# Moving the first expert's down product ahead of the slots' names and the third gather

## What is computed

```python
def hier_moe(x, w_group, w_router, w_gate, w_up, w_down):
    g_logits = (xt @ w_group)                      # 4 groups, the best one is taken
    ...
    e_top, e_idx = lax.top_k(e_logits, 2)          # 2 of its 8 experts
    e_w = jax.nn.softmax(e_top, axis=-1) * g_w
    ...
    hid = jax.nn.silu(xblk @ w_gate[e]) * (xblk @ w_up[e])      # 1024 -> 512
    return hid @ w_down[e]                                      # 512 -> 1024
```

## Time and profile before

| | us |
|---|---|
| median of 3 runs | 1673.22 (1672.76 to 1675.41) |
| profiled execution, own time | 1668.99 |
| its span | 1667.0 |
| TensorE busy | 1592.2 (96%) |
| VectorE busy | 486.2 (29%) |
| ScalarE busy | 356.8 (21%) |

### The profile page before, as it was taken

How to read it: one execution, slowest core, us unless ns; L and a number is a source line. 1 busy time by engine, 2 the same in 40 slices (tenths; PEclk the granted TensorE clock), 3 DMA queues, 4 the chain that set the end, 5 groups by cost and what they waited for, 6 DMA issues and landing times.

```text
span 1667.0 us, 21128 instructions
## 1 busy us (share of the span) xinstructions
PE 1592.2 (96%) x7988; PEld 754.5 (45%) x7988; DVE 486.2 (29%) x1252; ACT 356.8 (21%) x835; POOL 197.6 (12%) x298
## 2 busy tenths in 40 slices
PE   7999899899999999999899989999899999999995
PEld 4545574433333333333446447865433333333332
DVE  1485751621111111111412235652611111111114
ACT  2445351301111111111200235642111111111110
POOL 2240320000000000000101012330000000000000
PEclk9999999999999999999999999999899999999998
DMA  8620217379999999999914120034699999999997
GB/s 239 254 100 7 85 21 303 134 299 421 422 422 421 421 422 423 422 422 400 348 14 173 66 54 1 1 138 166 254 416 422 421 421 422 422 422 421 422 422 314
DMA packets 118312, 474.20 MB, mean 284 GB/s; under 512 B 40821, under 2 KB 47221, under 8 KB 68332
## 3 DMA queue, kind: packets, MB, share of 16 engines
q1 hardware_dynamic: 110156, 456.98, 68.5%
q10 hardware_dynamic: 3136, 8.40, 1.3%
q0 software_dynamic: 4960, 8.04, 1.3%
HBM read 454.84 MB, written 26.77 MB: 289 GB/s over the span
## 4 chain that ended last, share of the span: by engine, by line
PE 75%; SPq 11%; DMA 5%; DVE 5%; issue 2%; ACT 1%; POOL 1%; DVEq 0%; POOLq 0%; ACTq 0%
PE bank L1845 19%; PE bank L1858 9%; SPq L1791 9%; PE bank L1473 8%; PE bank L1818 8%; PE bank L550 7%; PE bank L844 6%; PE bank L438 4%; DMA arena<-in_moe_w_up 3%; PE bank L403 3%; PE bank L1833 2%; SPq L1800 2%; PE bank L925 2%; PE bank L420 2%; DVE arena L2354 1%
## 5 line engine op out<-in xcount | busy, mean ns | idle before, releaser
L1845 PE MATMUL bank<-arena 128*64 128x512 f32 x2048 | 454.3, 596 | 9.3 <-DMA arena<-in_moe_w_up 5.8
L1845 PEld LDWEIGHTS bank<-arena 128*64 128x64 f32 x2048 | 144.2, 138 | 306.7 <-issue 293.6
L1858 PE MATMUL bank<-arena 128*64 128x512 f32 x1024 | 230.6, 592 | 2.1 <-DVE arena L1951 2.1
L1947 DVE TENSOR_TENSOR arena<-arena,bank 128x256 f32<-128x256 f32 x64 | 26.9, 421 | 644.5 <-ACT arena L1937 644.5
L1818 PE MATMUL bank<-arena 128*64 128x512 bf16 x1280 | 164.8, 388 | 1.9 <-DVE arena L1813 1.9
L1864 POOL DMA_INDIRECT y_d<-arena,slot_row x62 | 60.7, 979 | 864.2 <-ACT arena L1942 837.0
L1473 PE MATMUL bank<-arena 128*128 128x512 f32 x320 | 138.1, 593 | 0.8 <-ACT arena L320 0.8
L1858 PEld LDWEIGHTS bank<-arena 128*64 128x64 f32 x1024 | 71.8, 137 | 124.2 <-issue 110.6
L1937 ACT ACTIVATE arena<-bank 128x256 f32<-128x256 f32 x64 | 24.5, 383 | 415.2 <-PE bank L1845 415.2
L550 PE MATMUL bank<-arena 128*128 128x512 f32 x256 | 111.9, 594 | 0.0
L844 PE MATMUL bank<-arena 128*128 128x512 f32 (+1 forms) x288 | 105.3, 525 | 0.0
(11 more groups left out here) (305 smaller groups left out, 1455.4 us busy)
## 6 DMA issues: line engine op xcount, KB each, us to landing
arena<-in_moe_w_gate SPq DMA_DIRECT2D x128, 1024.0 KB, 20.1
arena<-in_moe_w_up SPq DMA_DIRECT2D x128, 1024.0 KB, 22.9
arena<-in_moe_w_down SPq DMA_DIRECT2D x62, 2048.0 KB, 24.4
arena<-in_even_w_in SPq DMA_DIRECT2D x4, 2048.0 KB, 8.1
y_d<-arena ACTq DMA_DIRECT2D x2, 4096.0 KB, 16.7
arena<-y_d SPq DMA_DIRECT2D x8, 1024.0 KB, 9.2
arena<-bias_row_d SPq DMA_DIRECT2D x2, 3584.0 KB, 11.9
arena<-in_odd_w_in SPq DMA_DIRECT2D x3, 2048.0 KB, 8.4
```

Of the source, the lines that this page charges most:

```text
L1845: mm = nc.tensor.matmul(bank[1][fh * CAP:(fh + 1) * CAP, :], xeT[:, j, half * CAP:(half + 1) * CAP], wgu[u][:, :, n, fh * FH:(fh + 1) * FH ...
L1858: mm = nc.tensor.matmul(bank[3][dh * CAP:(dh + 1) * CAP, :], hidT[:, j, fh * CAP:(fh + 1) * CAP], wd[u][:, n, dh * 512:(dh + 1) * 512], st ...
```

## The change

In the opening of each layer's experts TensorE's order changes from gather 1, names, rows' turn 1, gather 2 (two parts), hidden turn 0, gather 2 (last part), down 0 to gather 1, hidden turn 0, rows' turn 1, down 0, names, gather 2. (Gather n is the one for expert n; gather 2 is the layer's third.) VectorE follows: `hid_out` comes ahead of `x_out`, and `name_rows` comes behind `x_out`, directly ahead of `further_rows`. ScalarE's, GpSimd's and SP's programs stay as they are.

```diff
                 gate_up(pe, t, c, cu, u)
                 if isinstance(c, int) and c == L * NE:
                     picked(pe, t, c + 1)
+                    hid_turn(pe, t, c)
+                    x_turn(pe, t, c + 1)
+                    down(pe, t, c, cu, u)
                     slot_names()
+                    picked(pe, t, c + 2)
+                    return
                 if after >= 1:
                     x_turn(pe, t, c + 1)
...
                 if after >= 2:
                     ones_for(dve, t, c + 2, e + 2)
                 if opening:
-                    name_rows()
+                    hid_out(dve, t, c)
                 else:
                     hidden(dve, t, c)
                 if after >= 1:
                     x_out(dve, t, L, c + 1)
                 if opening:
+                    name_rows()
                     further_rows()
-                hid_out(dve, t, c)
+                else:
+                    hid_out(dve, t, c)
```

## The result

| | before | changed |
|---|---|---|
| median, first comparison (19 and 19 runs), us | 1672.11 | 1677.39 |
| median, second comparison (35 and 12 runs), us | 1672.52 | 1675.85 |
| ratio with its 95% interval, first and second | | 1.0035 [1.0027, 1.0043] and 1.0021 [1.0010, 1.0032] |
| profiled execution's own time and span, us | 1668.99, 1667.0 | 1677.32, 1675.4 |

The change makes the kernel slower by some 5 us (5.8 and 3.5 by the two ratios). I had +2.1 us. The direction and the place were right; the size was a third of the first ratio's and 0.6 of the second's. Against its own base, 1672.11, the first comparison's +5.3 lies above the range that I gave (up to +4.2).

A forecast was written before the change was run, and what follows sets the result against it. Weight transfers were taken to bound each layer's end. A slightly later issue, a shorter start-up and 1.24 us of moved bytes gave +1.08 and +1.06 us, +2.1 in all: 1675.3 us from a 1673.22 median, range 1673.0 to 1677.4.

The forecast's parts named there:

- What bounds the kernel: Each layer's end: weights land last, so it is the opening hole's end plus all bytes still to come, at 422 GB/s.
- TensorE's part: Each layer's opening: TensorE idles about 0.3 us before the rows' turn; next gate and up 0.38 us later, costing nothing.
- Who is queued: SP's queue in the opening: held at the routing's count until 355.54, so down, 4.2 us earlier, releases nobody early.
- The sum: Hole's end in each layer: later issue, start-up and 512 KB behind the hole give +1.08 and +1.06 us, +2.1 in all.
- start-up term: Restart after the hole: two issues in a row take 1.56 us until data flows effectively, against 1.80 for a single one.
- later release: SP's issue that sets the hole's end in layer 0: at 355.54 in place of 355.46.
- bytes: Expert 2's last 512 KB of down weights now flow behind the hole: 1.24 us a layer at 422 GB/s.
- In turn: Hole's end: the small down transfer lands before the large one flows; +2.1 us a layer, +4.2 in all, 1677.4; chance 0.12.
- Hidden: Hole's end: the 512 KB disappear in the large transfer's start-up; +0.4 us a layer, 1674.0; chance 0.14.
- SP isn't held: SP's queue: names out before down ends, so the hole fills; gain capped at 0.3 us a layer, 1672.6; chance 0.04.
- Chances and range: Whole kernel: forecast band 1674.8 to 1676.0 us had chance 0.66; range 1673.0 to 1677.4.
- last waits longer, about 1.4 for 0.65: Layer's end, experts 30 and 31: TensorE's last waits for up weights grow to about 1.4 us from 0.65.

The follow-up runs named there:

- f2: The kernel before with all of expert 2's down weights (2048 KB, three transfers) issued after the wait for expert 0's down, ahead of expert 3's; ratio 1.0060, +10.0 us.
- e1: The changed kernel with SP issuing expert 3's down weights first, and only then waiting for the routing and issuing expert 2's last 512 KB; ratio 0.9988, -2.0 us.
- e3: The changed kernel without loading the last 512 KB of expert 2's down weights, SP raising the count instead; ratio 1.0000 to before.
- e0: The changed kernel again, with no edit, for a second profile; ratio 1.0021 to before, +3.5 us.
- e2: The kernel before with expert 2's last 512 KB issued after the wait for expert 0's down, directly ahead of expert 3's 2048 KB; ratio 1.0016, +2.7 us.
- f1: The kernel before with expert 2's last 512 KB issued behind expert 3's 2048 KB, both after the wait for expert 0's down; ratio 1.0024, +4.0 us.
- g1: The changed kernel with SP issuing expert 3's 2048 KB first and expert 2's 512 KB behind them; ratio 1.0015 to before, +2.5 us.
- g3: The changed kernel with expert 3's down weights issued before the routing wait and expert 2's last 512 KB, run again; ratio 0.9992 to before.

## Why the prediction was wrong

**What bounds the kernel: right.** The end of each layer follows the transfers. f2 shows it most plainly: bytes moved behind the hole, and nothing else, cost 4.8 us a layer of an expected 4.97; e1 and e3 take all or nearly all of the loss away without touching TensorE.

**TensorE's part: right in kind, 0.12 short.** 0.38 us later was forecast, 0.50 came; the idle time in front of the rows' turn was 0.25 for 0.3. It cost nothing, as said: e1 has it and is under before.

**Who is queued: right.** SP stood at the routing's count for 11.1 us, and the down product, 4 us earlier, released nobody. The release came 0.22 us behind before's issue (11.99 for 11.77); I had 0.08. In e3, where the release stands alone, this term is 0.3 us a layer.

**The sum: its start-up term failed.** I took 1.56 us for the start of two issues in a row, from a pair of 1024 KB transfers, as if it held for any pair, and so credited the change with 0.24 us a layer. The row was the wrong neighbour: it leads with a large transfer. Reckoned in the same way from the windows shown above, the start took 3.41 us in layer 0 of the changed kernel (2325 KB until 365 us, so effectively from 359.49 for an issue at 356.08), 3.19 in e0, and 1.78 in layer 1. There the term itself was up to 1.9 us too low. At the last landing the order of the pair, small first against large first, makes 1.0 and 0.8 us a layer between e2 and f1, 1.8 and 1.3 in layer 0 and 1.5 and 0.6 in layer 1 between the changed kernel's two profiles and g1. The terms as measured, a layer: later release 0.3 (forecast 0.08), bytes 1.24 (f1: 1.24; forecast 1.24), small transfer in front about 1.2 (0.6 to 1.8; forecast -0.24). Their sum, 2.7, times two is 5.4; the changed kernel's four distances are 2.7 over before in the mean. That agreement is in part built in, as four of the six differences use those distances; with e2 and f1 alone the term is 0.9 and the sum 4.9. By times alone the term isn't shown: the changed kernel is above g1 (+5.8 and +3.5 against +2.5), but e2 is below f1 (+2.7 against +4.0).

**A second fault stands behind the first.** I read the start from GB/s, which is a mean over 16 engines, and the sum had no term for the engine that lands last. In e2, where the start was ordinary (1.71 and 1.91 us), the extra price is all there. A mean can't bound that term from above. Whether the last engine picks its lateness up in the restart isn't shown: e2's layer 0 goes from a spread of 1.4 us to 9.1, e3's from 2.7 to 8.3.

**The rivals.** "In turn" named a price close to the true one (+2.1 a layer, +4.2) for a mechanism that wasn't there: in four of the six layers with the small transfer directly ahead the start took 1.58 to 1.91 us (1.58 in layer 1 of e0), where "in turn" wants 3.8; and f1, with both in the same place, costs the bytes only by its distances. Layer 0 of the changed kernel, with 3.41 and 3.19, comes near it in size, but there too the two overlap: the large one's first 8 KB packets start 2.5 us behind the small one's issue, and in e0 the small one lands at 3.8 us only. "Hidden" (+0.4) is refuted by f1 and f2. "SP isn't held" was what e1 built: -0.65 and -0.3 us (means of e1 and g3), where I had capped it at 0.3 a layer.

**Chances and range.** Half of the forecast's chance should have gone to a dearer start: the windows of the earlier trace rows had different starts, 1.56 and 1.80, and I had no row with a small transfer in front. The signature "last waits longer, about 1.4 for 0.65" was wrong in form: TensorE begins to wait two experts earlier, and each wait stays near 1 us; my reading is that a wait makes TensorE itself late and so shortens the next. Expert 31's in layer 0 even fell, from 1.39 to 1.22.

The 358 GB/s of the Trainium skill (DMA: Bandwidth & Descriptors, Specifications) gave an estimate of +2.6 us. That it came nearer is luck: the rate stayed 422 GB/s in every long window, and the missing time lay elsewhere.

## What to carry to other kernels

Where a queue of loads runs without a hole to the end of a stage, the stage ends at the last hole's end plus the bytes still to come: every byte that a reordering moves from inside a hole to behind it is paid in full, and a product finished earlier gains nothing if the queue that it should release stands at another wait. Before moving a step, write down, for each queue that waits on it, what that queue waits for just ahead. After a hole, try the large transfer first: here it never cost anything by the distances, and it saved 0.6 to 1.8 us a layer in six comparisons of single profiles.

## What the runs showed of the hardware

The 16 DMA engines drift apart while all are full: the reports of one 2048 KB load are 0.5 to 2.9 us apart at the start of a layer and 7.4 to 9.6 us apart 400 us later, so a load's last landing comes up to about 5 us behind the mean of its 16 (e2, layer 1: 437.3 for 432.3). When they run dry at the end of a layer the windows show it. Before:

```profile
784.00:788.00 4.00, 2.94 (x14) 0.86 (x10) 0.00 (x0) 0.00 (x0) 0.35 (x1) 1.00 0.85 356
788.00:792.00 4.00, 3.65 (x16) 1.06 (x16) 0.00 (x0) 0.00 (x0) 0.00 (x0) 1.00 0.70 247
```

The share falls to 0.70 while the down weights of expert 31 are still under way (their last report comes at 793.42 us). A restart behind a hole of 4 us can be slow for 8 us (146 and 319 GB/s in two windows of 5 us). Both profiles of the changed kernel had it in layer 0, with the small transfer first; layer 1 of both and both layers of e2 had not, with the same order, and none had it with the large one first. And TensorE's clock comes up from 1.2 to 2.4 GHz (granted 0.50 and 1.00) at different moments of a layer's first gate and up product: it took 7.09 us in nine of 28 openings, 8.78 or 8.79 in sixteen, and 8.41, 9.99 and 10.03 in one each, behind 1.4 to 2.0 us of idle time in all of them. That is up to 2.9 us a layer of the spread between executions.
